# Where the second layer's modulation products run: block 1, or the norms, feed-forward ends and first attention

## What is computed

```python
silu_c = jax.nn.silu(c)
for i in range(2):
    mod = silu_c @ ada_w[i] + ada_b[i]           # 1024 x 6144 per layer
    sh1, sc1, g1, sh2, sc2, g2 = split(mod, 6)
    h = rms_norm(x, norm_mix_g[i]) * (1 + sc1) + sh1
    x = x + g1 * attention_i(h)                   # i = 0: 8 heads, two maps each; i = 1: 16 heads
    h = rms_norm(x, norm_ffn_g[i]) * (1 + sc2) + sh2
    x = x + g2 * experts_i(h)                     # 16 experts, 2 per row
```

## Time and profile before

| | |
|---|---|
| median of three runs | 1241.11 us (1240.93 to 1243.22) |
| the profiled execution | 1244.53 us, its span 1242.7 us |
| TensorE busy | 1129.1 us (91%), granted clock 0.98 of full on average |
| VectorE busy | 592.3 us (48%) |
| ACT busy | 436.5 us (35%) |
| moved by transfers | 354.04 MB, 285 GB/s on average |

### The profile page before, as it was taken

One profiled execution on the slowest core, in us unless ns is written; L12 is line 12 of the kernel. 1 busy time (PEld: TensorE's weight loads), 2 busy tenths in 40 slices (PEclk: granted clock), 3 DMA queues, 4 the chain that ended last, 5 costly groups with the idle time before them and its releaser, 6 DMA issues.

```text
span 1242.7 us, 17517 instructions
## 1 busy us (share of the span) xinstructions
PE 1129.1 (91%) x6864; PEld 753.3 (61%) x6864; DVE 592.3 (48%) x1174; ACT 436.5 (35%) x746; POOL 78.5 (6%) x157
## 2 busy tenths in 40 slices
PE   6899978889999998997999998988999999999986
PEld 5677545579999996875754343423787864343422
DVE  3268454456766666748522322224774542333223
ACT  5344613254445446537331110103554541120100
POOL 2112133100000000002000000000000000000000
PEclk9999988899999999998999999998999999999999
DMA  9998898546677772583479999997476379999995
GB/s 293 366 296 282 293 349 319 193 136 195 193 223 219 232 220 87 169 287 122 154 284 410 409 409 409 409 409 271 170 246 262 111 275 411 409 408 409 409 409 237
DMA packets 162957, 354.04 MB, mean 285 GB/s; under 512 B 9912, under 2 KB 78776, under 8 KB 162752
## 3 DMA queue, kind: packets, MB, share of 16 engines
q1 hardware_dynamic: 146864, 295.81, 65.5%
q0 software_dynamic: 16000, 57.16, 13.0%
q10 hardware_dynamic: 16, 0.02, 0.0%
HBM read 351.89 MB, written 7.36 MB: 289 GB/s over the span
## 4 chain that ended last, share of the span: by engine, by line
PE 72%; DMA 15%; DVE 8%; ACT 3%; issue 1%; POOL 0%; DVEq 0%; SPq 0%; ACTq 0%
PE bank L552 37%; PE bank L1103 12%; DMA ering<-in_moe_w_up 9%; PE bank L1114 8%; DMA ering<-in_ada_w 5%; PE bank L499 3%; PE bank L1071 3%; PE bank L822 1%; DVE wlo L542 1%; PE bank L1763 1%; PE bank L849 1%; PE bank L1175 1%; DMA a_raw<-in_ada_w 1%; PE bank L1796 1%; PE bank L1876 1%
## 5 line engine op out<-in xcount | busy, mean ns | idle before, releaser
L542 DVE TENSOR_TENSOR wlo<-wraw,whi 128x1024 fp32r<-128x1024 f32 x150 | 179.5, 1221 | 67.1 <-ACT whi L538 64.6
L538 ACT ACTIVATE whi<-wraw 128x1024 fp32r<-128x1024 f32 x150 | 153.7, 1055 | 68.3 <-PE bank L552 49.0
L552 PE MATMUL bank<-a_hi,whi 128*128 128x256 f32 x512 | 148.4, 290 | 4.4 <-DVE a_lo L739 2.4
L1103 PE MATMUL bank<-ering,work 128*64 128x512 f32 x592 | 134.8, 596 | 14.6 <-DMA ering<-in_moe_w_up 11.2
L552 PE MATMUL bank<-a_lo,whi 128*128 128x256 f32 x512 | 146.3, 286 | 0.0
L552 PE MATMUL bank<-a_hi,wlo 128*128 128x256 f32 x512 | 146.2, 286 | 0.0
L1304 DVE TENSOR_TENSOR work<-work,bank 128x512 f32<-128x512 f32 x16 | 11.0, 688 | 212.1 <-PE bank L1103 212.1
L552 PEld LDWEIGHTS bank<-a_hi,whi 128*128 128x128 f32 x512 | 99.6, 195 | 17.9 <-issue 13.3
L552 PE MATMUL bank<-whi,a_hi 128*128 128x512 f32 x256 | 102.4, 400 | 5.8 <-DVE a_lo L739 3.0
L1103 PEld LDWEIGHTS bank<-ering,work 128*64 128x64 f32 x592 | 40.8, 137 | 106.3 <-issue 78.0
L1212 ACT ACTIVATE o_hi<-work 128x512 fp32r<-128x512 f32 x32 | 20.2, 631 | 236.6 <-DVE work L1272 236.2
(11 more groups left out here) (312 smaller groups left out, 1821.1 us busy)
## 6 DMA issues: line engine op xcount, KB each, us to landing
ering<-in_moe_w_down SPq DMA_DIRECT2D x44, 1024.0 KB, 18.4
ering<-in_moe_w_up SPq DMA_DIRECT2D x42, 1024.0 KB, 18.5
ering<-in_ada_w POOLq DMA_DIRECT2D x80, 512.0 KB, 6.2
ering<-in_moe_w_gate SPq DMA_DIRECT2D x32, 1024.0 KB, 18.2
work<-in_moe_w_gate SPq DMA_DIRECT2D x16, 1024.0 KB, 16.7
wraw<-in_w_in SPq DMA_DIRECT2D x28, 512.0 KB, 8.0
wraw<-in_a_w_qkv SPq DMA_DIRECT2D x24, 512.0 KB, 4.6
work<-in_moe_w_down SPq DMA_DIRECT2D x12, 1024.0 KB, 18.5
```

The source lines that it names most:

```text
L538: nc.scalar.activation(w_hi(c), wraw[:, c % RING, :], ACT.Copy).then_inc(w_hi_done, 1)
L542: nc.vector.tensor_tensor(w_lo(u[0]), wraw[:, u[0] % RING, :], w_hi(u[0]).bitcast(F32), ALU.subtract).then_inc(w_lo_done, 1)
L552: mm = nc.tensor.matmul(out_ap, l, r, start=first and n == 0, stop=last and n == len(terms) - 1)
L1103: mm = nc.tensor.matmul(bank[rows, :], x_e[:, k, rows], w[:, e, kk * HALF:(kk + 1) * HALF], start=first and kk == 0, stop=last and kk == 1)
```

## The change

- The groups' order becomes (0,2), (0,0), (0,1), (1,2), (1,0), (1,1): layer 0 first. Block 1 keeps the 24 bundles of layer 0: 6 in its attention (`SIDE_BUNDLES`), 2 at the z units, 6 up to the levels, 2 in each of the five full levels.
- The 24 of layer 1: 3 after the output projection in place of the 18 filling products; one after each of the feed-forward's first three steps; 2 before its last down unit; 8 after it, in the norm; and one after each of the first eight turns of layer 0's attention in place of the 10 filling products behind it. They use other places (parts of `work`, and expert places 10 to 14), and banks 7, 2, 3, 7.
- Layer 0's column products move from before the levels to after the output projection, layer 1's to after layer 0's attention. The router's shift is made per layer, layer 1's inside its q, k, v units.
- The rows of gates come by transfers: POOL issues 16 copies per layer (`mod_spread`) of 32 x 512 from `grow` to `mrow`. The products at L1862 and ACT's copies go, with the 11 filling products of layer 0; those of layer 1 stay.
- In layer 0's attention bank 6 alone serves the value products, so `values(i - 3)` now comes before `largest(i)`, and TensorE waits for each head's finished rows before the next head's values.
- The turn before the feed-forward uses banks 4 to 7 and waits for x. SP waits for bundle 34 before the bias rows, and loads expert piece 0 of layer 0 after the last two units of w_o, once the column products are done.

```diff
-ADA_GROUPS = [(0, 2), (1, 2), (0, 0), (0, 1), (1, 0), (1, 1)]
+ADA_GROUPS = [(0, 2), (0, 0), (0, 1), (1, 2), (1, 0), (1, 1)]
-ADA_BANK = 7
-ADA_LATE = 24
+ADA_BANK = [7, 7, 7, 2, 3, 7]
+ADA_LATE = 12
+ADA_BLOCK = 24
+ADA_TAIL = [0, 1, 2, 0, 1, 2, 0, 1, 2, 10, 11, 12, 0, 1, 2, 10, 12, 13, 14, 12, 13, 14, 12, 13]
+ADA_PLACE = [n % (2 if n < ADA_LATE else 3) for n in range(ADA_BLOCK)] + ADA_TAIL
+ADA_NORM, ADA_STEP, ADA_LASTS, ADA_FFN = 27, 30, 32, 40
+SIDE_BUNDLES = [1, 1, 2, 2, 3, 3, 4, 4, 5, 6]
...
         def load_ada(pool, n):
+            if ada_turn(n) > 1:
+                pool.wait_ge(ada_used, max(m for m in range(n) if ada_ring(m) == ada_ring(n)) + 1)
...
-            return psum[6] if ph == 0 else psum[6 + n % 2]
+            return psum[6] if ph < 2 else psum[6 + n % 2]
...
-                    if ph == 0 and n >= 1:
+                    if ph < 2 and n >= 1:
                         pe.wait_ge(att_y, u0 + n)
...
-                if ph == 0 and i >= 3:
+                if ph < 2 and i >= 3:
                     values(i - 3)
...
-                for r in range(7):
+                if l == 1:
+                    expert_load(0)
+                for r in range(1, 7):
                     expert_load(r)
                 load_square(w_o, U_WO[l], range(RING, KC))
+                if l == 0:
+                    expert_load(0)
...
+            def mod_spread(l):
+                for n in range(4):
+                    for q in range(4):
+                        nc.gpsimd.dma_start(mrow[32 * q:32 * q + 32, n // 2, (n % 2) * HALF:(n % 2 + 1) * HALF],
+                                            grow[l][32 * n:32 * n + 32, :]).then_inc(mod_rows, 16)
...
             nc.gpsimd.memset(fg[:, :, 0:2], 0.0).then_inc(pads_zero, 1)
+            for n in range(ADA_BLOCK, ADA_STEP):
+                load_ada(pool, n)
+            pool.wait_ge(grow_done, 1)
+            mod_spread(0)
+            for n in range(ADA_STEP, ADA_STEP + 6):
+                if ADA_PLACE[n] == 10:
+                    pool.wait_ge(w_used, U_FFN)
+                load_ada(pool, n)
...
+            for n in range(ADA_STEP + 6, ADA_FFN + 1):
+                load_ada(pool, n)
             toe_mask(0)
+            pool.wait_ge(w_used, U_WO[0])
+            for n in range(ADA_FFN + 1, ADA_FFN + 5):
+                load_ada(pool, n)
             for n in range(SUB_POOL):
                 pool.wait_ge(att_y, ATT_U[1] + n + 1)
...
+                if ADA_FFN + 5 + n < ADA_N:
+                    load_ada(pool, ADA_FFN + 5 + n)
...
             mod_columns(psum[3])
-            busy(psum[0], BUSY_NORM)
+            ada(ADA_NORM)
+            pe.wait_ge(x_done, X_AT["wout"])
             turn_pe(pe, 2, hn_done, 4)
             step_pe(pe, 0, None, 0, turn=2)
+            ada(ADA_NORM + 1)
             step_pe(pe, 1, None, 0, first=True)
+            ada(ADA_NORM + 2)
             step_pe(pe, 2, None, 0)
+            ada(ADA_STEP)
...
             step_pe(pe, FF_STEPS - 1, None, 0)
+            ada(ADA_LASTS)
             down_pe(pe, FF_STEPS - 1, None, 0, last=True)
+            ada(ADA_FFN)
...
-                for n in range(4):
-                    nc.tensor.matmul(psum[n][:, :], con[:, C_SEL + n:C_SEL + n + 1].to_broadcast([P, P]), grow[l][:, :],
-                                     start=True, stop=True).then_inc(mod_ps, 1)
-                busy(psum[4], BUSY_MOD)
+                if l == 1:
+                    busy(psum[4], BUSY_MOD)
...
-                attention_pe(pe, 1 + l)
+                attention_pe(pe, 1 + l, None, (lambda i: ada(min(ADA_FFN + 1 + i, ADA_N))) if l == 0 else None)
                 if l == 0:
-                    busy(psum[0], BUSY_Y)
+                    pe.wait_ge(acol_done, 4)
+                    mod_columns(psum[7])
```

More of the change, by code:

```diff
@@ L438, in build_program @@
         sil_c = sem("sil_c")
-        ada_in = [sem(f"ada_in{b}") for b in range(3)]
+        ada_in = [sem(f"ada_in{b}") for b in range(6)]
         ada_used, grow_done, acol_done = sem("ada_used"), sem("grow_done"), sem("acol_done")
@@ L464, in load_unit, with ada_ring, ada_turn, ada_part @@
             sp.dma_start(dst, src).then_inc(raw_in[c % RING], 16)
-        def ada_slot(n):
-            if n < ADA_LATE:
-                return n % 2, n // 2
-            return n % 3, (n - ADA_LATE) // 3 + (ADA_LATE // 2 if n % 3 < 2 else 0)
+        def ada_ring(n):
+            return {10: 3, 11: 4, 12: 5, 13: 3, 14: 4}.get(ADA_PLACE[n], ADA_PLACE[n])
+        def ada_turn(n):
+            return [ada_ring(m) for m in range(n + 1)].count(ada_ring(n))
+        def ada_part(n, h):
+            place = ADA_PLACE[n]
+            if place >= 3:
+                return eplace(place)[:, h, :]
+            return ada_at[place][h] if n < ADA_BLOCK else wk((2 * place + h) * UNITW, UNITW)
         def load_ada(pool, n):
@@ L983, in attention_dve @@
                     between(i)
-                if ph != 0 and i >= 3:
+                if ph == 2 and i >= 3:
                     values(i - 3)
@@ L1500, in _ @@
                     sp.wait_ge(att_y, ATT_U[2])
-                sp.wait_ge(skew_a_out if l == 0 else skew_b_out, 16 * (A_H if l == 0 else B_H))
+                sp.wait_ge(skew_out, 16 * (A_H + B_H))
                 heads = A_H if l == 0 else B_H
+                if l == 0:
+                    sp.wait_ge(ada_used, max(n for n in range(ADA_N) if ADA_PLACE[n] == 11) + 1)
                 for h in range(heads):
@@ L1680, in side_bundles @@
                 if i < len(SIDE):
-                    ada(8 + SIDE_END[i])
+                    ada(SIDE_BUNDLES[i])
             pe.wait_ge(g_evac, 8)
@@ L1688, in _ @@
                 unit_columns(pe, (U_Z + j, None, 0), j, psum[4:6])
-                ada(21 + j)
+                ada(min(7 + j, 8))
                 if j == 1:
@@ L1706, in _ @@
                 mm.then_inc(g_ps, 1)
-            ada(25)
+            ada(9)
             pe.wait_ge(silu_done, 3)
@@ L1717, in _ @@
                 tr.then_inc(vtr_ps, 1)
-                ada(26 + c)
+                ada(10 + c)
             pe.wait_ge(qk_unit, 4)
@@ L1722, in _ @@
             tr.then_inc(vtr_ps, 1)
-            ada(28)
+            ada(12)
             for c in range(2):
@@ L1735, in _ @@
                 mm.then_inc(kk_ps, 1)
-            ada(30)
+            ada(13)
             for c in range(2):
@@ L1743, in _ @@
                 tr.then_inc(m1_ps, 1)
-            ada(32)
+            ada(14)
             def mod_columns(bank):
@@ L1775, in _ @@
                     blocks(psum[3 * c + 2], nm[c], xm[c]).then_inc(xyn_ps, 1)
-                ada(32 + 2 * n)
+                ada(14 + 2 * n)
             lo, up = BLOCKS
@@ L1784, in _ @@
                 mm.then_inc(n_ps, 1)
-            ada(31 + 2 * LAST)
             for c in range(2):
@@ L1791, in _ @@
                 mm.then_inc(xyn_ps, 1)
-            ada(32 + 2 * LAST)
             def heads(bank, l, r, signal):
@@ L2478, in _, with router_weights @@
                 ffn_step(s_)
-            dve.wait_ge(crow_ps, 1)
-            nc.vector.tensor_copy(sm[:, M_CR:M_CR + 32], psum[3][:, 0:32])
-            for l in range(2):
+            def router_weights(bank, l):
+                dve.wait_ge(crow_ps, l + 1)
+                nc.vector.tensor_copy(sm[:, M_CR + 16 * l:M_CR + 16 * l + 16], bank[:, 0:N_EXP])
                 for k in range(KC):
@@ L2550, in _ @@
                     splits(U_WO[0] + 1)
+                    modulation(1, psum[7])
                     invert(dve, or_done, 3, M_OR, 16)
```

133 lines of the change are left out of this document (59 added, 74 removed).

## The result

The changed kernel takes **1238.78 us** in the median (1235.44 to 1241.78), the kernel before, run beside it, 1242.92 (1238.91 to 1247.7): ratio 0.9963, with an interval of 0.995 to 0.9975. So it is faster, by 4.1 us; 22.5 were forecast, and the time lies above the range, which ended at 1235. The profiled executions have spans of 1242.7 and 1236.8 us, 5.9 apart.

The account below looks back on a forecast made before the run. TensorE's time, bundles and waits for them included, was taken to bound block 1. Removing 35 us there and adding 12.5 elsewhere nets 22.5; 1244.5 less 22.5 and 3.4 (profiled run to median) gives about 1218 us, range 1203 to 1235.

Parts of the forecast that it names:

- Before the attention, "11 us": Block 1 before its attention: eight bundles leave, 8.0 us, and about 3 us of TensorE's idle time before bundles; 11 us won.
- Attention and z "8" and up to the levels "7": Block 1: 8 us (3 to 12) won in attention and z units, 7 us from there to the levels.
- Levels and closing, "9": End of block 1: levels give 7.5 us (3 to 11) as bundles and waits go, closing products 1.5 of 4.
- Fillers for bundles at the first norm, "1 us": Norm before the feed-forward: three bundles replace 18 filling products, TensorE stands a little longer before step 0; 1 us (0 to 3) added.
- The norm after the feed-forward, "1 us (0 to 4)": Eight bundles fit before hn's turn, TensorE reaching hn about as it is written; 1 us (0 to 4) added.
- The order in layer 0's attention, "1.2 us in each of six heads, 0.5 at the end": Layer 0's attention: VectorE, adding values before the next scores, waits for TensorE's value products; 7.2 us plus 0.5 added.
- Loads in the same attention, "1.5 us for bundle 42": Layer 0's attention: loads 41 and 42 issued together with the experts' loads; TensorE may wait 1.5 us for bundle 42.
- bundles late by some 6 us in all: Rival for layer 0's attention: bundles 41 to 47 share full transfer engines with the experts' loads; 1224 us, chance 0.08.
- Layer 1, "3 us won, 1.8 returned": Layer 1: row products that delayed hn's turn go, 3 us won; the router's product returns inside the units, 1.8 us.
- VectorE's and ACT's chains carry block 1: Rival: in block 1 these engines' chains take back the waits, so 35 us won shrink to 20; 1233 us, chance 0.17.
- the last rival (1241): Rival: the change doesn't do what it says, block 1's gains lost to an unseen wait of POOL's queue; 1241 us, chance 0.02.
- The places set the pace: Rival for layer 0's attention: bundle loads wait for freed places, a head costing 11 us instead of about 3; 1266, chance 0.04.

## Why the prediction was wrong

The direction was right, and most of the terms. Four failed, all in one direction, by 20 us together: the two of block 1 up to the levels (26 foretold, 17.5 measured), the norm after the feed-forward (1, 6.0) and layer 0's attention (9, 16.0). They have one root: a load was priced as the wait of one bundle, not as a share of full queues. In layer 0's attention it is the 1.5 us for bundle 42 that failed; the 7.7 us for the order were nearly of the right size, for a wrong reason. The other rows came out 4 us better than foretold, which is why the total misses by 16 (by the table) and not by 20.

- **Before the attention, "11 us": 8.4.** I read the idle time of TensorE as waits before bundles that would go with them. With the bundles gone TensorE arrived sooner at unit 6, whose load was late, and stood 4.7 instead of 2.1 us. I had looked at VectorE's and ACT's busy time as the bound, and not at the queues, which rows 2 show full (share 1.08). Two loads and eight bias rows that no longer had a use there cost 6.6 us.
- **Attention and z "8" and up to the levels "7": 9.1 of 15.** VectorE's turn is the bound in the attention, as said. But "waits for ada under 8 us" measured 12.8, step 0 began at 251.55 and not "near 244", and without any loads it begins 17.9 us sooner. These are loads over two or three places, which stay short of time with half the bundles.
- **Levels and closing, "9": 10.2.** Right, within the spread of this stretch.
- **Fillers for bundles at the first norm, "1 us": 0.2**, and the low clock named there is what happened in this execution: the turn took 3.64 us at half clock.
- **The norm after the feed-forward, "1 us (0 to 4)": 6.0.** The step that failed is "the fastest load of the rows (5.3 us)" for bundle 38 from 474.2. The place came free when I said, 4.4 us after the last down unit began (3.9 foretold); the load did not take 5.3 us. Loads 36 and 37 are issued from 443.9 on, 38 and 39 from 448.7 on, they take 7.8 to 9.6 us and land one per 2.6 us, some 400 GB/s, the rate of the full queues in the stretches above. "A norm of layer 0 that ends on bundle 39 and not on hn", a sign of being wrong, is what came. Places freed earlier gave all of it back (11.5 us against 11.3 before). The fit of the Trainium skill (DMA: Bandwidth & Descriptors, the anatomy of one DMA), some 4.4 us per bundle as an estimate, made this term zero. The trace does not agree where several loads are under way (7.8 to 9.6 us); the nearest to it is 4.9 to 5.2 us for half a bundle in the attention with the experts' pieces held.
- **The order in layer 0's attention, "1.2 us in each of six heads, 0.5 at the end": 11 us alone by the ratio, 13.7 in the profiled execution.** It was eight heads, and 1.3 us at full and 2.3 at half clock. And I took the order as needed by the single bank. It was not: the wait was VectorE's place in its own iteration. Restored, it gave 6.2 us of the 16 with late loads, 10.0 with loads in time.
- **Loads in the same attention, "1.5 us for bundle 42": 8.2** once the order is restored, 4.4 with the new one. I had made this a rival of 0.08, "bundles late by some 6 us in all". Its mechanism is right and belonged in the sum. The attention took 51.8 us to w_o, 43 to its last value product: "an attention of over 45 us" was a sign of being wrong, 38 the forecast.
- **Layer 1, "3 us won, 1.8 returned"**: right. Two more came between the experts' start and the last x (224.6 and 222.7 us); no run asks why.
- **The rivals.** "VectorE's and ACT's chains carry block 1" (1233) comes nearer in time than the forecast, by luck: without loads these chains let block 1 shrink by another 18 us. Nearest is the last rival (1241), that the gains of block 1 are lost again. It had the place wrong: block 1 kept its 27.5 us, and they were lost behind it. "The places set the pace", the slower one, did not occur: heads were 4.5 us apart and not 11, and with the experts' pieces held TensorE took a bundle every 3.0 to 3.4 us in the middle of the attention, with no wait above 0.2 us.

## What to carry to other kernels

When work with large loads moves, price it by the queues at the new place: what is queued there, bytes over the measured rate, and which of the loads is needed last. What a load takes between issue and landing depends on the transfers beside it, so a row read in one stretch doesn't price another. Early loads that served the old place keep costing after the work has left it; look for them in the first full stretch. And where an order of VectorE was chosen for a buffer, check in the waits of both engines whether the buffer really asks for it, before counting a wait per head.

## What was not expected of the hardware

- Two costs in one stretch hid each other: order 6.2, loads 4.4, both 14.3 us of 51.8.
- A half-clock stretch nearly doubled a cost that is small by itself: the same wait of VectorE for three products was 1.31 us at full clock and 2.28 at half, and the column products took 3.41 us instead of 1.89.
- Six pieces of 1 MB, issued 30 us and more later where the queues were empty before, cost nothing, and their early issue had cost 8 us elsewhere.
- The same code took 44.6 to 50.2 us for levels and closing products in ten profiles. A single pair of profiles can show 5 us there that no edit made.
